# First modulation of a two-layer attention block: the order of its loads, and who sums the context side's shift

## What is computed

```python
mod_x = silu(c) @ ada_w + ada_b          # one row, 3 x 1024: shift, scale, gate
mod_c = silu(c_ctx) @ ada_w + ada_b      # the same for the context side
h  = rmsnorm(x,   norm_w) * (1 + scale)   + shift
hc = rmsnorm(ctx, norm_w) * (1 + c_scale) + c_shift
p  = h @ w_in                            # then hc @ w_in[:, :KV_COLS], attention, gates, output
```

## Time and profile before

| | |
|---|---|
| three runs, median (lowest to highest) | 1743.93 us (1743.3 to 1746.08) |
| the profiled execution's own time | 1746.52 us |
| its span | 1744.7 us |
| TensorE busy, matmuls | 1674.3 us (96%) |
| VectorE / ScalarE / GpSimd busy | 1026.2 (59%) / 1067.9 (61%) / 625.9 us (36%) |
| chain that ended last, by engine | TensorE 75%, VectorE 11%, ScalarE 9% |
| DMA | 129.5 MB, mean 74 GB/s; 322 GB/s over the first fortieth (43.6 us) |
| the ninth 0.5 MB load, as TensorE waits for it; rate from 20 to 23 us | 17.18 us; 407 GB/s |
| end of VectorE's last shift pass | 28.65 us |
| mean granted clock of TensorE | 0.99 of full |

### The profile page before, as it was taken

How to read it: one execution, slowest core, us unless ns; L and a number is a source line. 1 busy time by engine, 2 the same in 40 slices (tenths; PEclk the granted TensorE clock), 3 DMA queues, 4 the chain that set the end, 5 groups by cost and what they waited for, 6 DMA issues and landing times.

```text
span 1744.7 us, 27026 instructions
## 1 busy us (share of the span) xinstructions
PE 1674.3 (96%) x10400; PEld 1467.7 (84%) x10400; DVE 1026.2 (59%) x2124; ACT 1067.9 (61%) x1984; POOL 625.9 (36%) x426
## 2 busy tenths in 40 slices
PE   6999999999999999999999999999999999999998
PEld 2878888889989889989889987788888887888788
DVE  6345766665565655554774635566676656565634
ACT  4535777766666777765321174677776677786333
POOL 1533333333333322322322263443343533443442
PEclk9999999999999999999999999999999999999999
DMA  9211111111121111111644423111122221212642
GB/s 322 52 38 29 26 47 37 49 32 49 50 55 38 43 43 43 37 43 43 208 148 157 133 73 77 41 38 47 49 51 67 77 62 42 61 49 67 199 151 97
DMA packets 178531, 129.51 MB, mean 74 GB/s; under 512 B 21658, under 2 KB 167652, under 8 KB 178404
## 3 DMA queue, kind: packets, MB, share of 16 engines
q1 hardware_dynamic: 174240, 115.36, 23.2%
q10 hardware_dynamic: 2884, 8.24, 1.3%
q0 software_dynamic: 1280, 4.20, 0.8%
HBM read 123.58 MB, written 4.19 MB: 73 GB/s over the span
## 4 chain that ended last, share of the span: by engine, by line
PE 75%; DVE 11%; ACT 9%; issue 3%; DMA 1%; POOL 0%; SPq 0%; POOLq 0%; DVEq 0%; ACTq 0%
PE acc L1405 55%; PE wide L1458 7%; PE ptp L1476 6%; PE pv L1489 4%; PE pv L1490 3%; DVE nmax L2092 2%; ACT e L1726 2%; DVE pt L2117 1%; DMA w_raw<-in_ada_w 1%; ACT w_hi L1643 1%; DVE k_m L1595 1%; DVE q_s L1595 1%; ACT k_m L1586 1%; DVE k_s L1595 1%; DVE lat_r L2005 1%
## 5 line engine op out<-in xcount | busy, mean ns | idle before, releaser
L1875 POOL TENSOR_TENSOR w_lo<-w_raw,w_hi 128x1024 fp32r<-128x1024 f32 (+2 forms) x192 | 391.5, 2042 | 560.9 <-ACT w_hi L1643 559.4
L1405 PE MATMUL acc<-h_hi,w_hi 128*128 128x512 f32 (+2 forms) x1320 | 465.0, 353 | 12.1 <-DVE lf L1995 4.7
L1405 PE MATMUL acc<-h_hi,w_lo 128*128 128x512 f32 (+2 forms) x1320 | 462.0, 351 | 0.0
L1405 PE MATMUL acc<-h_lo,w_hi 128*128 128x512 f32 (+2 forms) x1320 | 458.3, 351 | 0.6 <-POOL h_lo L1937 0.6
L1405 PEld LDWEIGHTS acc<-h_hi,w_hi 128*128 128x128 f32 (+1 forms) x1320 | 249.9, 189 | 50.5 <-issue 12.4
L1741 ACT ACTIVATE pt<-ptp 128x512 fp32r<-128x512 f32 (+3 forms) x312 | 165.7, 563 | 198.5 <-PE ptp L1476 196.8
L1405 PEld LDWEIGHTS acc<-h_hi,w_lo 128*128 128x128 f32 (+1 forms) x1320 | 249.6, 189 | 33.5
L1405 PEld LDWEIGHTS acc<-h_lo,w_hi 128*128 128x128 f32 (+1 forms) x1320 | 246.9, 189 | 34.8 <-POOL h_lo L1937 1.0
L2092 DVE TENSOR_REDUCE nmax<-wide 128x1 f32<-128x768 f32 (+3 forms) x240 | 190.0, 792 | 107.5 <-PE wide L1458 104.1
L1929 POOL TENSOR_TENSOR o_t<-o_half,o_t 64x256 f32<-64x256 f32 x120 | 92.2, 768 | 436.4 <-DVE o_half L2124 434.4
L1733 ACT ACTIVATE e<-e,einv 128x768 f32<-128x768 f32 (+3 forms) x240 | 193.5, 806 | 57.1 <-DVE einv L2109 56.7
(11 more groups left out here) (228 smaller groups left out, 3073.9 us busy)
## 6 DMA issues: line engine op xcount, KB each, us to landing
w_raw<-in_w_in SPq DMA_DIRECT2D x102, 512.0 KB, 3.9
w_raw<-in_ada_w SPq DMA_DIRECT2D x48, 512.0 KB, 5.3
w_raw<-in_w_out SPq DMA_DIRECT2D x16, 512.0 KB, 3.6
w_raw<-in_w_in SPq DMA_DIRECT2D x16, 256.0 KB, 3.2
w_raw<-in_w_o_mla SPq DMA_DIRECT2D x16, 256.0 KB, 2.8
w_raw<-in_w_o_swa SPq DMA_DIRECT2D x16, 256.0 KB, 2.8
w_raw<-in_w_o_ax SPq DMA_DIRECT2D x16, 256.0 KB, 2.8
w_raw<-in_mla_w_uq SPq DMA_DIRECT2D x16, 144.0 KB, 2.4
```

The costliest lines, as they stand in the source:

```text
L1405: ins = nc.tensor.matmul(dst, lhs, rhs, start=first, stop=last)
L1875: nc.gpsimd.tensor_tensor(w_lo[s][:, 0:k], w_raw[s][:, 0:k], f(w_hi[s][:, 0:k]), ALU.subtract).then_inc(w_lo_ready, 1)
```

## The change

The loads of shift and scale chunks now alternate, and the first two row tiles load behind the fourth pair (before: behind the sixth scale chunk, as position 15 of the queue). The shift of side x stays on VectorE, in `ptp`, with its last pass into `x_mod[:, 1]`. The context side's shift is made by two other engines: ScalarE scales each chunk with that side's column (in place; the first goes to `fin_w`), GpSimd adds the seven others to `fin_w`. Each event is now `AS`, ahead of the `AF` of the same number. Tiles a and b are squared ahead of the seventh pair; a is normed and turned between the seventh `AS` and its `AF`. All six tiles of the first layer are normed on VectorE. The modulation of a and b stands ahead of the second `W` and of the squares of c and d, and the context side's small products stand behind the turn of tile d.

```diff
-        for third in (0, 0, 0, 1, 0, 0, 1, 0, 1, 0, 1, 0, 1, 1, 1, 1):
-            if third == 0:
-                sums.append(shift_row(len(sums)))
-            else:
-                scale.append(chunk("adr", 0, 1, len(scale), (0, 1), slot=FIRST[KD + len(scale)]))
...
+        for third in (0, 1, 0, 1, 0, 1, 0, 1, 0, 1, 0, 1, 0, 0, 1, 1):
+            k = len(rows[third])
+            rows[third].append(chunk("adr", 0, third, k, (0, 1), slot=FIRST[third * KD + k]))
...
         for k in range(KD):
-            run_all(sums[k])
-            emit("AF", c=scale[k], k=k)
+            n["ad"] += 1
+            emit("AS", c=shift[k], k=k, n=n["ad"])
             if k == 2:
                 emit("VT")
             if k == KD - 3:
                 emit("VC")
-            if k == KD - 2:
                 for tt in (a, b):
                     square_rows(0, tt, 0)
-        for tt in (a, b):
-            norm_rows(tt, by="v")
+            if k == KD - 2:
+                norm_rows(a)
+                turn_rows(a)
+            emit("AF", c=scale[k], k=k)
+        norm_rows(b)
         emit("AC")
-        run_all(shift_sums((0,)))
-        turn_rows(a)
+        go(shift_sums(0))
         emit("AT")
         turn_rows(b)
         emit("W", c=early[0])
-        for tt in (c, d):
-            square_rows(0, tt, 0)
-        emit("W", c=early[1])
-        n["split"] = early[1] + 1
-        norm_rows(c)
         emit("MOD", l=0, free=n["free"])
         n["mod"] += 1
         modulate_rows(a)
-        norm_rows(d)
-        other_side, read_other = shift_sums((1,), defer=True)
-        run_all(other_side)
-        turn_rows(c)
         modulate_rows(b)
+        emit("W", c=early[1])
+        n["split"] = early[1] + 1
+        for tt in (c, d):
+            square_rows(0, tt, 0)
+        for tt in (c, d):
+            norm_rows(tt)
+            turn_rows(tt)
+        modulate_rows(c)
         load_table("s")
-        turn_rows(d)
-        modulate_rows(c)
-        read_other()
+        go(shift_sums(1))
...
-    def norm_rows(tt, by="a"):
-        emit("XN", tt=tt, n=row_of[tt], by=by)
+    def norm_rows(tt):
+        emit("XN", tt=tt, n=row_of[tt], by="v" if row_of[tt] < TT else "a")
...
-                if chunks[c][:4] == ("adr", 0, 1, KD // 2 + 1):
+                if chunks[c][:4] == ("adr", 0, 1, KD // 2 - 1):
...
+                elif ev == "AS":
+                    c, k = e["c"], e["k"]
+                    if new(ada_used, e["n"]):
+                        act.wait_ge(ada_used, e["n"])
+                    raw = w_raw[slot_of[c]][:, :]
+                    dst = raw if k else first_shift(1)[:, :]
+                    nc.scalar.activation(dst, raw, ACT.Copy, scale=cs_n[:, k, 1:2]).then_inc(side_scaled, 1)
...
+                elif ev == "AS":
+                    c, k = e["c"], e["k"]
+                    if k:
+                        if new(side_scaled, k + 1):
+                            pool.wait_ge(side_scaled, k + 1)
+                        if new(side_added, k - 1):
+                            pool.wait_ge(side_added, k - 1)
+                        total = first_shift(1)[:, :]
+                        nc.gpsimd.tensor_tensor(total, total, w_raw[slot_of[c]][:, :], ALU.add).then_inc(side_added, 1)
...
+                    total, raw, column = ptp[:, 0:D], w_raw[slot_of[c]][:, :], cs_n[:, k, 0:1]
+                    if k == 0:
+                        nc.vector.tensor_scalar(total, raw, column, None, ALU.mult).then_inc(ada_used, 1)
+                    else:
+                        dst = total if k < KD - 1 else first_shift(0)
+                        nc.vector.scalar_tensor_tensor(dst, raw, column, total, ALU.mult, ALU.add).then_inc(ada_used, 1)
```

## The result

The changed kernel takes 1756.01 us (median of four runs, 1753.51 to 1757.47), the kernel before beside it 1744.07 us: a ratio of 1.0062, 95% interval [1.0049, 1.0075]. It is slower, by 11.9 us where 5.7 were forecast, and outside the range given. The profiled execution of the changed kernel took 1753.51 us (span 1751.7), the fastest of its four, while that of before (1746.52) was slower than all four runs of that kernel, so the two traces differ by 7.0 us only.

The account below looks back on a forecast made before the run. TensorE was taken as the bound almost everywhere, the change touching only what precedes its steady work. +3.4 + 5.0 − 2.7 = +5.7 us on the median 1743.9 gave 1749.6 us, range 1744.8 to 1752.0.

Parts of the forecast that it names:

- A: End of the scale products, at the copy of the scale sums (`a_row`): 31.1 us before, 34.5 forecast.
- Part 1: Opening up to A: TensorE waits for the vector rows' turn and loses clock; +3.4 us.
- Part 2: A to the first projection: held xn copies, slow turns and small products ahead make 13.5 us into 18.5; +5.0.
- the 16 small products 1.9: Context side's products on TensorE, moved ahead of the first projection: 1.9 us charged within Part 2.
- Part 3: First projection to the long run: ScalarE, freed of xn copies, follows at once; 17.8 us becomes 15.1, −2.7.
- the last wait: TensorE's stand just before the long run: 1.8 us instead of 2.3; 1.7 us of lost clock may stay or be saved.
- the long run: TensorE's long run of projections: started at 62.34 us before, forecast at 68.0; its shift taken one to one into the time.
- the mark: Not forecast: last of four squares of the first projection's latent rows on ScalarE; 78.33 us before, 86.59 changed.
- Costed at nothing: Opening: ScalarE's scalings, GpSimd's additions, accumulation passes beside GpSimd and VectorE's second xn, all taken to add no time.
- Rival 2: Not slower: TensorE isn't late at A, which stays at 31.1; 1744.5 us, or 1742.8 with clock kept; chance 0.17.
- Rival 1: One link missing: xn not held (+3.9), clock kept before A (+4.1), or both (+2.3); chance 0.29.
- Rival 3: Worse: clock low for longer behind the vector rows' turn or again at the end; +8.3, 1752.2 us; chance 0.04.

Follow-up runs that it names:

- vt_back: The changed kernel with the turn of the vector rows back behind the third scale product; ratio to the kernel before 1.0068.
- turn_back: The changed kernel with the vector rows' turn behind the third scale product, row a's turn and both first norms behind the last; ratio to before 1.0037.
- fill_short: The changed kernel with 36 useless products on TensorE behind row b's turn, to fill its pause; ratio to the kernel before 1.0052.
- again: The changed kernel timed and traced once more, no edit; 1754.54 us, ratio to the kernel before 1.0063.
- tab: The changed kernel with cosine and sine tables loaded ahead of the first weight split and scaled behind row b's modulation; ratio to the kernel before 1.0065.
- loads_only: The kernel before with nothing but the changed load order; ratio to the kernel before 0.9997.
- as_only: The kernel before with the changed loads and division of the shift sums (ScalarE scales, GpSimd adds), every order as before; ratio to before 0.9996.
- before_v: The kernel before with all normalized copies on VectorE (rows c and d and both context rows moved there), nothing else; ratio to before 0.9988.

## Why the prediction was wrong

The direction and the place were right: TensorE late at A, then late for row c. What failed is the price of two terms behind the stand, because the low clock was charged on the turns only, and one comparison.

- **Part 1 (+3.4).** A at 34.76 is +3.66: right. The vector rows' turn ran at 18.66 (18.9 taken), after an idle of 3.28 us, and the clock was 0.60 from 18 to 22 us. But the cause was half told. I had written that the tile is ready "sooner than the queue gets there (about 30)", with 1.7 us to spare, and left out that this makes row a's turn the next bound: vt_back gained nothing, turn_back the whole 3.8.
- **Part 2 (+5.0).** The copies were right: row c's held (2.75 us), d's done at A+14.1 (14.4 forecast), turn c at A+13.3. The failed term is "the 16 small products 1.9": that is their time at full clock, and they stood behind a stand of 9.9 us and took 3.41; the two turns took 1.76 and 1.71 from start to start where I had 1.5 (the row that I read it from gives 1.60). First projection at A+20.0 instead of A+18.5: 1.5 us. With the clock at full (fill_short) they took 0.93, 0.87 and 1.71.
- **Part 3 (−2.7).** The failed term is "24 + 24 products ... at 2.88 per 24". From 54.78 to the context turn at 62.96 they took 8.18 us, not 5.76, at a clock of 0.51 from 50 to 60: 2.4 us. In fill_short, at full clock, they took 5.8. I had ScalarE's tail right: from there on, 0.87 + 2.88 + 0.87 and then the last wait, TensorE went on 4.6 us after ScalarE began the last context tile (67.61 to 72.20). In all 17.4 us instead of 15.1.
- **The clock.** Both are one omission. I charged a lost clock ahead of A and behind the last wait, and at the longest stand, which my own numbers put at 10 us, only on the turns. The kernel before had 0.69 from 38 to 42 us, around its first short stand, and turns at half pace behind it; that the level could last into a block of products I didn't follow up. How long it lasts is partly luck: 11.7 us of work in the changed kernel, 11.4 in again, 3.4 and 3.5 in turn_back and tab. Why it differs is open.
- **The sum.** At the long run 0.3 + 1.5 + 2.3 = 4.1 us are missing: 5.7 forecast, 9.86 in the trace. Behind it 1.6 came back (the last wait was 1.77 us and the clock stayed at 1.00, one of the two ways I had left open), so 8.3 at the mark.
- **From the trace to the median.** I put the difference on both, since "the sum is a difference". The profiled execution of before was 2.6 us above its median and had lost 1.7 us behind the long run, which loads_only and as_only, equal to it in time, had not. Against a mark of 76.6 the changed kernel is 10 us late, near the 10 to 12 us of the medians. That most runs of before don't pay that drop is argued from these two kernels, not shown for before itself. What differs further on is not settled either; it goes with the clock: among the 11 runs of before beside again, the fastest (1742.86) had a mean granted clock of 0.994 and the slowest (1750.18) of 0.988.
- **Costed at nothing.** ScalarE's scalings and GpSimd's additions: right (as_only). The tables were not in my list at all. Their hold (4.65 us instead of 0.97) was hidden by the slow clock here and became the bound as soon as the clock was mended. So part 3 would have been too small in any case: with the clock as full as I took it, it was 17.9 us instead of 15.1.
- **Rivals.** Rival 2 fell (TensorE was late at A). Rival 1 too: both links were there. Rival 3 had a longer low clock, but behind VT or at the end, where neither was: behind VT it was what I had charged, and behind the last wait it stayed full. It had 8.3 us at 0.04, and the 8.3 at the mark match it by luck. No rival had the low clock behind the stand of 10 us, and with that stand in the forecast one should have.

## What to carry to other kernels

If a forecast makes TensorE stand for long, price the work behind the stand at the low clock too, as a bound, not only the wait. When work is moved ahead in a queue, look for the next bound directly behind the one you name; removing one of two equal bounds gains nothing, and an experiment must remove both. When the parts that you undo add up to the loss, look for a gain that hides another part. And a relief of an engine that the path doesn't wait for is worth nothing: look in the change for what is freed in passing on the engine that the path does wait for.

## What the runs showed of the hardware

- Behind a stand of 9.9 us the granted clock was 0.51 over 50 to 60 us of unbroken work; in again, behind the same stand, the stretch had 0.61, in turn_back 1.00, and in tab, behind 10.7 us, the 16 small products at 50.95 took 1.87 us, the time of full clock. Stands of 2.35 and 2.36 us, with the same order of work on TensorE ahead, were followed by a drop in one execution and by none in the other.
- A VectorE copy of 128x1024 in SBUF takes 0.75 us alone and 0.8 to 2.9 us beside GpSimd; a 128x512 scaling goes from 0.48 to 2.0 and 2.6. The added time is about the rest of the running GpSimd instruction (2.35 us each): held copies ended 0.55 us after it in the changed kernel (47.99 against 47.44) and three times in before_v (35.81, 39.59, 48.67 against 35.26, 39.04, 48.11). The second scaling waited for the next one too. VectorE's passes into PSUM kept their 1.27 to 1.29 us beside GpSimd's additions.
